# Hybrid decoder step: no drain of gathers between the later stages, 80 candidate sums instead of 256 in routing, and 24 gathered items moved between stages

## The chip, the cores and the metric

The kernel runs on one core of one Trainium2 chip. The metric is device time in microseconds (us) of one execution. The core has five engines: PE (matrix products), DVE (vector work), ACT (scalar work and activations), POOL (GpSimd; here it issues the gathers) and SP (here it only issues transfers). All transfers share the core's 16 DMA engines.

## The reference, cut to what matters

One decoder layer over 560 tokens (32 sample, 16 meta, 512 prompt), all in float32. The part before the experts is a norm, a large projection, eight gated-delta heads and eight attention heads, and an output projection. Then comes PEER, a retrieval of single experts, and most of the time goes there:

```python
qry = (xi @ w_query).reshape(PEER_BLOCK, PEER_HEADS, 2, PEER_HALF)
s = jnp.einsum('thpc,pnc->thpn', qry, sub_keys)
s1, i1 = lax.top_k(s[:, :, 0], PEER_TOPK)             # 16 of 128
s2, i2 = lax.top_k(s[:, :, 1], PEER_TOPK)
cand = (s1[..., :, None] + s2[..., None, :])          # 16 x 16 sums
cidx = (i1[..., :, None] * PEER_KEYS + i2[..., None, :])
top_s, pos = lax.top_k(cand, PEER_TOPK)               # 16 of 256
idx = jnp.take_along_axis(cidx, pos, axis=-1)
gate = jax.nn.softmax(top_s, axis=-1)
hid = jax.nn.gelu(jnp.einsum('td,thkd->thk', xi, expert_u[idx]), approximate=False)
return jnp.einsum('thk,thkd->td', (gate * hid), expert_v[idx])
```

Each token reads, for each of 8 heads, 16 rows of `expert_u` and 16 rows of `expert_v`, each row 2048 float32. Since the kernel works on 128 tokens at once, one *item* is one gather of 128 rows of 8 KB (1 MB) and one pass of DVE over it.

## The kernel before

The tokens are worked in two groups: `FIRST` (tag a, two tiles of 128 tokens) and `LATER` (tag b, tiles of 128, 128 and 48). Each group goes through the same five stages in `front`: `norm_and_gates`, `heads`, `mix_out` (output projection), `ffn_norm` and `route`. After `LATER`'s `route`, `rest_of_experts` does what is left of the experts.

A stage is a block in which each engine has its own instruction stream, ordered by semaphores. At the end of a block all engines meet; then `phase`'s `clear` resets the stage's semaphores, one barrier of all engines for each run of neighbouring numbers. `nc.Block()` ends with a drain on POOL: POOL waits there for the transfers that it has issued.

The experts are 1088 items, kept by `Stream` in a fixed order: 448 belong to tokens of `FIRST` (their indices are `known` once `FIRST` is routed), 640 to those of `LATER`. An item of kind u multiplies the gathered rows with the token's vector and sums them (L1919); an item of kind v adds the weighted rows to the result (L1934; the first of a set is L1930). POOL issues gathers (L1841) into a ring of `RING` = 6 buffers: `Stream.gather` runs up to six items ahead of what DVE has been given, and before each one waits until the buffer's last item has been consumed.

The 448 known items are spread over the stages of `LATER`. The table `OVERLAP` says how many each stage takes, and `Share` divides a stage's quota evenly over its steps: norm 14 items in 3 steps (one a tile), heads 330 at even marks of its written order, out 48 in 24 steps (8 column groups by 3 tiles), ffn 8 in 3 steps, route 48 in 32 steps (8 heads by 4 parts). `share.take` puts the items of a step into DVE's stream at that place, so all DVE work behind them waits for them. With `FIRST` there is no stream (`NONE`).

`mix_out`: PE makes a 256-column group of one tile (L2017) and DVE adds it to the residual (L2044); weights of `out_b_w` come in pieces of 2 MB, two buffers. The last gather of each stage waits for the last item of the stage, so POOL always ends a stage with up to six gathers under way.

`route`, for each of 8 heads: PE projects the queries (L2203) and scores them against 128 keys, twice (L2211); ACT copies queries and scores out of PSUM. `top16` finds the best 16 on DVE by MAX8, FIND_INDEX8 and MATCH_REPLACE8, eight at a time. Its first use is on 128 scores; the second is on the 256 sums `cand` (L2280). Then the index of each of the 16 winners is looked up by comparing its row and its column number with 0 to 15 (`iota`), multiplying with the index table `atf` and summing (L2294, L2297, L2299), and the gate is a softmax whose exponential is on ACT (L2237). ACT works in order: after the scores of a head it waits for `centred`, the middle of DVE's work on that head, before it copies the next head's queries.

Of the kernel before, what the change touches and what calls it, by code (L numbers as in the profile page):

```python
# [22 lines left out]
ALU = mybir.AluOpType  # L23
# [6 lines left out]
P = 128  # L30
# [69 lines left out]
def constant_parts():  # L100
    r = np.arange(P)
    row, col = r[:, None], r[None, :]
    mixed = FIRST.rows[0]
    seq0 = np.where(r < NS, r // NQ, np.where(r < mixed, NB, -1 - r))
    same0 = (seq0[:, None] == seq0[None, :]) & (r < mixed)[:, None]
    upto, after = [(row <= col) & same0, row <= col], [(row > col) & same0, row > col]
    levels = [((row // b) % 2 == 1) & (col // b == row // b - 1) for b in LEVELS]
    first_keys = np.arange(mixed - NS)[None, :]
    parts = {
        "upto": np.concatenate(upto, 1),  # L110
        "after": np.concatenate(after, 1),
        "not_upto": np.concatenate([np.where(m, 0.0, NEG) for m in upto], 1),
        "not_after": np.concatenate([np.where(m, 0.0, NEG) for m in after], 1),
        "levels": np.concatenate(levels[:1] + [m.T for m in levels[1:]], 1),
        "ident": row == col,
        "ones": np.ones((P, P)),
        "causal": np.where(col > row, NEG, 0.0),
        "members": seq0[:, None] == np.arange(NB + 1)[None, :],
        "iota": np.broadcast_to(np.arange(TOPK)[None, :], (P, TOPK)),
        "eps": np.full((P, 1), EPS),  # L120
        "eps_q": np.full((P, 1), EPS * HD),
        "row": row,
        "valid": row < LATER.rows[-1],
        "causal_mixed": np.where((row >= NS) & (first_keys > row - NS), NEG, 0.0),
        "causal0": np.where(same0 & (col <= row) | (row >= NS), 0.0, NEG)[:, :NS],
        "batch_cols": np.broadcast_to((np.arange(NS)[None, :] // NQ == np.arange(NB)[:, None]).reshape(1, -1),
                                      (P, NB * NS)),
    }
    return {k: np.asarray(v, np.float32) for k, v in parts.items()}
# [60 lines left out]
def build(nc, ins, outs):  # L190
    with ExitStack() as ctx:
# [21 lines left out]
        def keep(stack, name, shape, dt=F32):  # L213
            mem[name] = stack.enter_context(nc.sbuf_tensor(name, shape, dt))
# [91 lines left out]
def norm_and_gates(nc, ins, outs, mem, scr, group, stream, quota):  # L306
    cst, xnT = mem["cst"], mem["xnT"]
    T, own, samples = group.n, group.own, group.samples
    ctx, sem, buf = phase(
        nc, f"norm_{group.tag}",  # L310
        "const_in first_in vec_rows_in narrow_in bias_in pages_in x_in0 x_in1 x_squared x_root x_scaled x_turned "
# [18 lines left out]
    with ctx:  # L330
# [245 lines left out]
def heads(nc, ins, outs, mem, scr, group, stream, quota):  # L576
# [15 lines left out]
    ctx, sem, buf = phase(  # L592
        nc, f"heads_{group.tag}",
        " ".join(f"w_in{s}" for s in range(W)) + " projected evacuated "
# [125 lines left out]
    with ctx:  # L720
        block = ctx.enter_context(nc.Block())

# [1239 lines left out]
def mix_out(nc, ins, mem, scr, group, stream, quota):  # L1962
# [11 lines left out]
    with ctx:  # L1974
# [3 lines left out]
        w_out = ins["w_out"][0].rearrange("(k p) c -> p k c", p=P)  # L1978
        block = ctx.enter_context(nc.Block())

# [68 lines left out]
def ffn_norm(nc, ins, outs, mem, scr, group, stream, quota):  # L2049
# [3 lines left out]
    ctx, sem, buf = phase(  # L2053
        nc, f"ffn_{group.tag}",
        "keys_in squared rooted reciprocals normed turned copied h_out xi_out0 xi_out1 keys_turned keys_copied",
# [6 lines left out]
    with ctx:  # L2062
        block = ctx.enter_context(nc.Block())

# [77 lines left out]
def route(nc, ins, mem, scr, group, stream, quota):  # L2142

    cst, xiT, skT = mem["cst"], mem["xiT"], mem["skT"]
    T, N = group.n, group.cols
    ctx, sem, buf = phase(
        nc, f"route_{group.tag}",
        "w_in0 w_in1 w_in2 w_in3 w_packed0 w_packed1 w_packed2 w_packed3 projected0 projected1 query_copied0 query_copied1 scored0 scored1 scores_copied0 scores_copied1 "
        "scores_read cleared dve_passed dve_order centred exped routed",
        {"w": ([P, 2, KT, P],), "q": ([P, 2, N],), "sc": ([P, T, 2, KEYS],), "top": ([P, T, 2, TOPK],),  # L2150
         "at": ([P, T, 2, TOPK], U32), "atf": ([P, T, 2, TOPK],), "cand": ([P, T, TOPK, TOPK],),
         "best": ([P, T, TOPK],), "pos": ([P, T, TOPK], U32), "pos2": ([P, 2, T, TOPK], U32),
         "posf": ([P, 2, T, TOPK],), "hot": ([P, T, TOPK, TOPK],), "pick": ([P, 2, T, TOPK],),
         "gate": ([P, T, TOPK],), "sum": ([P, T],), "rec": ([P, T],)},
        {"pq0": [P, BANK], "pq1": [P, BANK], "ps0": [P, BANK], "ps1": [P, BANK]},
# [14 lines left out]
    with ctx:  # L2170
        block = ctx.enter_context(nc.Block())

# [69 lines left out]
        def _(dve):  # L2242
# [26 lines left out]
            for h in range(HEADS):  # L2269
                order = Counter(dve, sem["dve_order"], h, 100)  # L2270
                share.take(dve, h * PARTS + 1)
                for s in range(2):
# [15 lines left out]

                order.mark(nc.vector.tensor_scalar(B.pos2[:, 0], B.pos[:], 4, None, ALU.logical_shift_right))
                order.mark(nc.vector.tensor_scalar(B.pos2[:, 1], B.pos[:], TOPK - 1, None, ALU.bitwise_and))  # L2290
                order.wait()
                order.link(nc.vector.tensor_copy(B.posf[:], B.pos2[:]))
                for s in range(2):
                    order.link(nc.vector.tensor_tensor(  # L2294
                        B.hot[:], B.posf[:, s].unsqueeze(3).to_broadcast([P, T, TOPK, TOPK]),
                        cst("iota").unsqueeze(1).unsqueeze(1).to_broadcast([P, T, TOPK, TOPK]), ALU.is_equal))
                    order.link(nc.vector.tensor_tensor(  # L2297
                        B.hot[:], B.hot[:], B.atf[:, :, s, :].unsqueeze(2).to_broadcast([P, T, TOPK, TOPK]), ALU.mult))
                    order.link(nc.vector.tensor_reduce(B.pick[:, s], B.hot[:], AX_X, ALU.add))  # L2299
                order.link(nc.vector.scalar_tensor_tensor(B.pick[:, 0], B.pick[:, 0], float(KEYS), B.pick[:, 1],  # L2300
                                                          ALU.mult, ALU.add))
                order.mark(nc.vector.tensor_copy(mem["idx_all"][:, group.own, h, :], B.pick[:, 0]))
                dve.wait_ge(sem["exped"], h + 1)
                order.link(nc.vector.tensor_reduce(B.sum[:], B.gate[:], AX_X, ALU.add))
                order.link(nc.vector.reciprocal(B.rec[:], B.sum[:]))
# [67 lines left out]
```

## Time and profile before

| | |
|---|---|
| runs | median 4594.33 us (4588.70, 4594.33, 4604.27) |
| profiled execution | 4603.0 us, span 4601.2 us |
| busy over the span | DVE 3369.4 us, PE 2388.2 us, POOL 2327.6 us, ACT 569.8 us |
| moved by DMA | 1513.69 MB, 329 GB/s over the span |
| group FIRST | start to 1200.7 us |
| group LATER, with 448 items beside it | 1201.7 to 2943.4 us |
| rest of the experts, 640 items | 2966.5 us to the end |

A row of a view has the duration of instructions in us or ns and, where a column says idle, how long the engine stood before them and who released it. An engine's idle time matters only where nothing else that is needed later was going on. DMA share is the mean busy share of the 16 DMA engines.

### The profile page before, as it was taken

To read this page: it belongs to the slowest core of one execution; us is meant where nothing else is said; L and a number is where in the kernel's file an instruction comes from. 1 tells how busy PE (TensorE), PEld (TensorE's weight loads), DVE (VectorE), ACT (ScalarE), POOL (GpSimd) and SP (SyncE) were. 2 spreads that over 40 slices of the span, in tenths; PEclk is the share of its full clock that TensorE was granted. 3 is DMA by queue.
4 is the path that set the end of the run, shared out by engine and by line. 5 is a ranking of instruction groups with operands and counts; after the bars stand their busy time and mean duration, and the time that the engine had idled before them with its cause. 6 is when DMAs were issued, how large, how long until landed. Compare 5 with 4: busy or idle time off the path is not lost. (4 is left out here: it accounts for less than half of the span.)

```text
span 4601.2 us, 35157 instructions
## 1 busy us (share of the span) xinstructions
PE 2388.2 (52%) x11713; PEld 1884.3 (41%) x11713; DVE 3369.4 (73%) x4421; ACT 569.8 (12%) x1322; POOL 2327.6 (51%) x1217
## 2 busy tenths in 40 slices
PE   6999999898488898888749555100000000000000
PEld 5888888777366666666537443000000000000000
DVE  2333323217779999989867589799998989999998
ACT  1222222201122222222200000000000000000000
POOL 1010101000246666545645222388887888888886
PEclk9999999899699999999869777555555555555555
DMA  6766666487779999999989764499999999999998
GB/s 176 225 202 191 198 202 207 149 287 230 273 278 401 401 397 412 400 381 399 372 337 419 265 234 184 173 420 422 418 422 396 414 414 422 422 417 418 413 412 353
DMA packets 443932, 1513.69 MB, mean 329 GB/s; under 512 B 42044, under 2 KB 276208, under 8 KB 277848
## 3 DMA queue, kind: packets, MB, share of 16 engines
q0 software_dynamic: 161840, 1158.85, 62.1%
q1 hardware_dynamic: 269240, 251.94, 17.2%
q10 hardware_dynamic: 12672, 100.67, 5.5%
q8 instruction: 93, 1.52, 0.1%
q14 instruction: 87, 0.71, 0.0%
HBM read 1384.96 MB, written 126.21 MB: 328 GB/s over the span
## 5 line engine op out<-in xcount | busy, mean ns | idle before, releaser
L1919 DVE CUSTOM_DVE_ANT_0 ex_ring<-ex_ring,ex_xi 128x2048 f32<-128x2048 f32 x544 | 1243.6, 2290 | 129.3 <-DMA ex_ring<-in_peer_u_dram,ex_idx_s 40.0
L1934 DVE SCALAR_TENSOR_TENSOR ex_y<-ex_ring,ex_wt,ex_y 128x2048 f32<-128x2048 f32 x538 | 1264.6, 2351 | 96.2 <-DMA ex_ring<-in_peer_v_dram,idx_all 53.7
L1841 POOL DMA_INDIRECT ex_ring<-in_peer_v_dram,idx_all x384 | 811.8, 2114 | 255.9 <-DVE ex_y L1934 138.2
L1841 POOL DMA_INDIRECT ex_ring<-in_peer_u_dram,idx_all x384 | 782.6, 2038 | 293.6 <-DVE ex_hid L1919 187.5
L848 PE MATMUL heads_b_pj<-xnT_b,lead 128*128 128x304 f32 x2048 | 604.4, 433 | 7.2 <-PEq L270 3.7
L1873 PE MATMUL ex_fold<-ex_y,const 128*32 128x512 f32 (+1 forms) x48 | 24.3, 670 | 1110.8 <-DVE ex_y L1934 1038.9
L1873 PEld LDWEIGHTS ex_fold<-ex_y,const 128*32 128x32 f32 (+1 forms) x48 | 6.2, 134 | 1128.4 <-DVE ex_y L1934 1039.8
L1841 POOL DMA_INDIRECT ex_ring<-in_peer_v_dram,ex_idx_s x160 | 303.0, 1894 | 296.0 <-DVE ex_y L1934 218.1
L1841 POOL DMA_INDIRECT ex_ring<-in_peer_u_dram,ex_idx_s x160 | 319.2, 1995 | 224.3 <-DVE ex_hid L1919 181.0
L848 PEld LDWEIGHTS heads_b_pj<-xnT_b,lead 128*128 128x128 f32 x2048 | 377.2, 197 | 119.4 <-issue 17.3
L848 PE MATMUL heads_a_pj<-xnT_a,heads_a_w 128*128 128x256 f32 x1216 | 316.6, 398 | 1.9 <-DMA heads_a_w<-in_w_in_dram 1.9
L848 PEld LDWEIGHTS heads_a_pj<-xnT_a,heads_a_w 128*128 128x128 f32 x1216 | 226.7, 199 | 32.3 <-issue 2.9
L1891 ACT ACTIVATE ex_act<-ex_hid 128x16 f32<-128x16 f32 x34 | 7.3, 216 | 1721.0 <-DVE ex_hid L1919 1720.9
L848 PE MATMUL heads_a_pj<-xnT_a,lead 128*128 128x256 f32 x832 | 214.9, 398 | 3.5 <-PEq L270 3.5
L1837 POOL DMA_DIRECT2D ex_xi<-xi_scratch x13 | 7.0, 549 | 380.6 <-POOLq L270 315.1
L848 PEld LDWEIGHTS heads_a_pj<-xnT_a,lead 128*128 128x128 f32 x832 | 156.3, 200 | 24.7 <-issue 5.8
L2017 PE MATMUL out_b_acc<-out_b_w,mixT_b 128*128 128x256 f32 (+1 forms) x672 | 147.4, 380 | 0.0
L2017 PEld LDWEIGHTS out_b_acc<-out_b_w,mixT_b 128*128 128x128 f32 (+1 forms) x672 | 111.5, 168 | 35.8 <-issue 5.1
L1663 POOL DMA_DIRECT2D out_k_prompt_dram<-heads_a_f_kN x16 | 8.9, 560 | 220.8 <-ACT heads_a_f_kN L1282 220.8
L1645 POOL TENSOR_TENSOR heads_a_ub<-heads_a_uN,const 128x1024 f32<-128x1024 f32 x8 | 15.3, 1914 | 191.1 <-ACT heads_a_uN L1239 191.1
L2017 PE MATMUL out_a_acc<-out_a_w,mixT_a 128*128 128x256 f32 x448 | 99.4, 384 | 6.7 <-DMA out_a_w<-in_w_out_dram 6.7
L1651 POOL DMA_DIRECT2D out_gdn_sample_dram<-heads_a_sout x8 | 7.6, 950 | 186.1 <-DVE heads_a_sout L1511 186.1
(566 smaller groups left out, 4023.8 us busy)
## 6 DMA issues: line engine op xcount, KB each, us to landing
lead<-w_scratch SPq DMA_DIRECT2D x64, 1024.0 KB
heads_a_w<-in_w_in_dram SPq DMA_DIRECT2D x38, 1024.0 KB, 6.1
w_scratch<-heads_a_w ACTq DMA_DIRECT2D x38, 1024.0 KB, 4.1
lead<-in_w_in_dram SPq DMA_DIRECT2D x26, 1024.0 KB, 5.8
w_scratch<-lead ACTq DMA_DIRECT2D x26, 1024.0 KB, 4.4
out_a_w<-in_w_out_dram SPq DMA_DIRECT2D x7, 2048.0 KB, 14.2
w_out_scratch<-out_a_w ACTq DMA_DIRECT2D x7, 2048.0 KB, 9.0
out_b_w<-w_out_scratch SPq DMA_DIRECT2D x7, 2048.0 KB, 12.7
```

Of the source, the lines that this page charges most:

```text
L848: last = nc.tensor.matmul(pj[j % PJ][:, 0:N], slot(j)[:, k, :], xnT[:, k, :], start=(k == 0), stop=(k == KT - 1))
L1645: nc.gpsimd.tensor_tensor(B.ub[:], B.uN[:, 0, :].unsqueeze(1).to_broadcast([P, NB, HD]), cst("members", 0, NB).unsqueeze(2).to_broadcast([ ...
L1651: pool.dma_start(outs["gdn_sample"][0, :, h].rearrange("b k v -> k b v"), B.sout[:]).then_inc(sem["gs_out"], 16)
L1663: pool.dma_start(out[place, h, :], rows[own_rows, t, :]).then_inc(sem[f"{own}_out{t}"], 16)
L1837: pool.dma_start(self.tokens(s)[part.on, :], self.xi_rows[part.xi_rows]).then_inc(self.sem["xi_in"], 16)
L1841: pool.indirect_dma_start(self.ring[:, i % RING, :], None, self.tables[which], bass.IndirectOffsetOnAxis(ap=self.index(s, g, k), axis=0)). ...
L1873: last = self.nc.tensor.matmul(self.fold[0:rows, c:c + BANK], self.mem["cst"]("ident", r * rows, (r + 1) * rows), self.sum_of(s)[:, c:c + ...
L1891: self.nc.scalar.activation(self.act[:, g % 2, :], self.hid[:, g % 2, :], ACT.Gelu).then_inc(self.sem["activated"], 1)
L1919: nc.vector.tensor_tensor_reduce(ring, ring, self.tokens(s)[:], 1.0, 0.0, ALU.mult, ALU.add, self.hid[:, g % 2, k:k + 1]).then_inc(self.se ...
L1934: nc.vector.scalar_tensor_tensor(y, ring, wt, y, ALU.mult, ALU.add).then_inc(self.sem["consumed"], 1)
L2017: last = nc.tensor.matmul(acc[0:b - a, i, 0:GW], mixT[:, k, a:b], weights[:, k, :], start=(k == 0), stop=(k == KT - 1))
```

## The change

Three edits. First, from the `LATER` group on (`mem["gathering"]`), stages end without POOL's drain and their semaphores are cleared by SP followed by one barrier on semaphores only. Second, `route` (in both groups) forms 80 sums instead of 256: the whole of row 0 (16), columns 0 to 7 of rows 1 to 7 (56), and column 0 of rows 8 to 15 (8). No other sum can be among the best 16, as the scores are sorted. A position among the 80 needs a little more arithmetic to become a row and a column; the table of row indices has 17 entries, the first of them twice. The copy of the indices to float moves to ACT (three copies), the softmax's subtraction and sum move into ACT's exponential (one per tile), and the index goes to `idx_all` directly. Third, the quotas: 12 items leave heads and 12 leave route; 8 go to norm, 12 to out, 4 to ffn.

```diff
-        "iota": np.broadcast_to(np.arange(TOPK)[None, :], (P, TOPK)),
+        "iota": np.broadcast_to(np.arange(TOPK + 1)[None, :], (P, TOPK + 1)),
...
         for a, b in zip(starts, ends):
-            nc.all_engine_barrier(sems_to_clear=range(a, b))
+            if gathering:
+                nc.sync.sem_clear(range(a, b))
+            else:
+                nc.all_engine_barrier(sems_to_clear=range(a, b))
+        if gathering:
+            nc.all_engine_barrier(sem_only=True)
...
-OVERLAP = {"norm": 14, "heads": 330, "out": 48, "ffn": 8, "route": 48}
+OVERLAP = {"norm": 22, "heads": 318, "out": 60, "ffn": 12, "route": 36}
...
-        block = ctx.enter_context(nc.Block())
+        block = ctx.enter_context(nc.Block(no_gpsimd_drain=mem["gathering"]))
...
-                act.wait_ge(sem["centred"], h + 1)
-                nc.scalar.activation(B.gate[:], B.gate[:], ACT.Exp).then_inc(sem["exped"], 1)
+                act.wait_ge(sem["scores_read"], h + 1)
+                if h >= 1:
+                    act.wait_ge(sem["picked"], h)
+                nc.scalar.copy(B.table[:, 0, :, 0:1], B.at[:, :, 0, 0:1])
+                nc.scalar.copy(B.table[:, 0, :, 1:], B.at[:, :, 0, :])
+                nc.scalar.copy(B.table[:, 1, :, 0:TOPK], B.at[:, :, 1, :]).then_inc(sem["tabled"], 1)
+                act.wait_ge(sem["best_found"], h + 1)
+                nc.scalar.mul(B.neg[:], B.best[:, :, 0], -1.0).then_inc(sem["negated"], 1)
+                act.wait_ge(sem["negated"], h + 1)
+                for t in range(T):
+                    last = nc.scalar.activation(B.gate[:, t, :], B.best[:, t, :], ACT.Exp, bias=B.neg[:, t:t + 1],
+                                                accum_out=B.sum[:, t:t + 1])
+                last.then_inc(sem["exped"], 1)
...
-                order.mark(nc.vector.tensor_copy(B.atf[:], B.at[:]))
-                order.link(nc.vector.tensor_tensor(B.cand[:], B.top[:, :, 0, :].unsqueeze(3).to_broadcast([P, T, TOPK, TOPK]),
-                                                   B.top[:, :, 1, :].unsqueeze(2).to_broadcast([P, T, TOPK, TOPK]), ALU.add))
-                top16(order, [(B.cand[rows[t], t].rearrange("p a b -> p (a b)"), B.best[rows[t], t, :], B.pos[rows[t], t, :])
-                              for t in range(T)])
-
-                nc.vector.tensor_tensor(B.gate[:], B.best[:], B.best[:, :, 0:1].to_broadcast([P, T, TOPK]), ALU.subtract
-                                        ).then_inc(sem["centred"], 1)
+                first, second = B.top[:, :, 0, :], B.top[:, :, 1, :]
+                order.mark(nc.vector.tensor_tensor(B.cand[:, :, 0:TOPK], first[:, :, 0:1].to_broadcast([P, T, TOPK]), second, ALU.add))
+                order.mark(nc.vector.tensor_tensor(
+                    B.cand[:, :, TOPK:72].rearrange("p t (a b) -> p t a b", b=8),
+                    first[:, :, 1:8].unsqueeze(3).to_broadcast([P, T, 7, 8]),
+                    second[:, :, 0:8].unsqueeze(2).to_broadcast([P, T, 7, 8]), ALU.add))
+                order.mark(nc.vector.tensor_tensor(B.cand[:, :, 72:CANDS], first[:, :, 8:], second[:, :, 0:1].to_broadcast([P, T, 8]),
+                                                   ALU.add))
+                order.wait()
+                if h >= 1:
+                    dve.wait_ge(sem["exped"], h)
+                top16(order, [(B.cand[rows[t], t, :], B.best[rows[t], t, :], B.pos[rows[t], t, :]) for t in range(T)])
+                dve.sem_inc(sem["best_found"], 1)
                 share.take(dve, h * PARTS + 3)
...
+                order.mark(nc.vector.scalar_tensor_tensor(B.last[:], row, 9.0, column, ALU.is_equal, ALU.mult))
+                order.mark(nc.vector.tensor_scalar(B.second[:], row, 1.0, 8.0, ALU.is_equal, ALU.mult))
+                order.wait()
+                order.mark(nc.vector.tensor_tensor(B.place[:, 0], row, B.last[:], ALU.add))
+                order.mark(nc.vector.tensor_tensor(B.place[:, 1], column, B.last[:], ALU.subtract))
+                order.wait()
+                order.link(nc.vector.tensor_tensor(B.place[:, 1], B.place[:, 1], B.second[:], ALU.add))
+                dve.wait_ge(sem["tabled"], h + 1)
```

The look-up behind it is as before, with 17 columns for the first index and 16 for the second; the copy to `idx_all` and the sum of the gates on DVE are gone.

## Rows read from the trace of the kernel before

**Rows 1.** The page: busy time of each engine over the span.

```profile
PE 2388.2 (52%) x11713; PEld 1884.3 (41%) x11713; DVE 3369.4 (73%) x4421; ACT 569.8 (12%) x1322; POOL 2327.6 (51%) x1217
```

**Rows 2.** Busy time in stretches: FIRST's route, norm, heads, drain, out, drain, ffn, drain, route, drain, tail.

```profile
core 0: us, PE busy (x) PEld busy (x) DVE busy (x) ACT busy (x) POOL busy (x), PEclk, DMA share, GB/s
1038.30:1200.70 162.40, 124.75 (x576) 107.65 (x576) 125.73 (x524) 15.22 (x57) 0.00 (x0) 0.91 0.64 207
1201.70:1274.50 72.80, 30.03 (x168) 27.43 (x169) 45.23 (x64) 11.30 (x16) 33.63 (x21) 0.55 0.89 342
1274.50:2358.40 1083.90, 904.61 (x4304) 656.36 (x4304) 977.99 (x1098) 270.08 (x588) 643.25 (x331) 0.93 0.95 384
2358.40:2376.80 18.40, 0.00 (x0) 0.00 (x0) 0.00 (x0) 0.04 (x1) 2.66 (x3) 0.50 0.68 285
2376.80:2553.10 176.30, 171.21 (x768) 129.38 (x768) 118.31 (x98) 1.67 (x3) 84.52 (x51) 0.98 0.97 395
2553.10:2565.10 12.00, 0.00 (x0) 0.00 (x0) 0.00 (x0) 0.00 (x0) 1.73 (x2) 0.51 0.49 180
2565.10:2599.90 34.80, 9.15 (x48) 8.33 (x48) 31.02 (x30) 7.96 (x10) 12.78 (x6) 0.55 0.79 294
2599.90:2611.50 11.60, 0.04 (x1) 0.07 (x1) 0.07 (x1) 0.00 (x0) 1.87 (x2) 0.50 0.73 271
2611.50:2943.40 331.90, 167.61 (x608) 119.53 (x608) 283.54 (x774) 20.39 (x76) 74.01 (x46) 0.74 0.50 181
2943.40:2966.50 23.10, 0.09 (x1) 0.12 (x2) 0.00 (x0) 0.00 (x0) 5.53 (x6) 0.50 0.77 315
...
3010.00:3500.00 490.00, 0.00 (x0) 0.00 (x0) 456.04 (x308) 1.29 (x6) 425.78 (x197) 0.50 1.01 421
```

**Rows 3.** DVE's u items and POOL's gathers: ns, minimum, median and maximum.

```profile
L1919 DVE CUSTOM_DVE_ANT_0 ex_ring<-ex_ring,ex_xi x544: 2266/2291/2366, 1211.2 to 4499.8; 128x2048 f32<-128x2048 f32 x182
L1841 POOL DMA_INDIRECT ex_ring<-in_peer_u_dram,idx_all x384: 932/2232/6452, 1203.1 to 4490.8; - x192
```

**Rows 4.** In order of time, from heads to out: start us, us, what, idle before.

```profile
2356.03 2.35 DVE L1934 SCALAR_TENSOR_TENSOR ex_y<-ex_ring,ex_wt,ex_y 128x2048 f32<-128x2048 f32 x1 [0.45 <-DMA ex_ring<-in_peer_v_dram,ex_idx_s]
...
2360.73 0.93 POOL L1841 DMA_INDIRECT ex_ring<-in_peer_v_dram,ex_idx_s  x1 [0.30 <-issue]
...
2376.95 23.22 PE L2017 MATMUL out_b_acc<-lead,mixT_b 128*128 128x256 f32 x93 [27.44 <-PEq L270]
```

**Rows 5.** The same, from route to the rest of the experts.

```profile
2949.51 0.94 POOL L1841 DMA_INDIRECT ex_ring<-in_peer_u_dram,idx_all  x1 [0.30 <-issue]
...
2966.52 2.29 DVE L1919 CUSTOM_DVE_ANT_0 ex_ring<-ex_ring,ex_xi 128x2048 f32<-128x2048 f32 x1 [23.13 <-PEq L270]
...
2993.31 2.29 DVE L1919 CUSTOM_DVE_ANT_0 ex_ring<-ex_ring,ex_xi 128x2048 f32<-128x2048 f32 x1 [0.15 <-DMA ex_ring<-in_peer_u_dram,idx_all]
```

**Rows 6.** DVE's instructions in LATER's route by shape: count, busy us, mean ns.

```profile
L2262 DVE FIND_INDEX8 route_b_at<-route_b_top,route_b_sc 128x8 uint32<-128x128 f32 x64 | 17.1, 285 | 0.0
L2262 DVE FIND_INDEX8 route_b_pos<-route_b_best,route_b_cand 128x8 uint32<-128x256 f32 x32 | 13.0, 419 | 0.0
```

**Rows 7.** In order of time, DVE in LATER's route: no wait ahead of the second, one ahead of the third.

```profile
2655.34 0.18 DVE L2289 TENSOR_SCALAR route_b_pos<-route_b_pos 128x48 uint32<-128x48 uint32 x1
2655.44 0.18 DVE L2290 TENSOR_SCALAR route_b_pos<-route_b_pos 128x48 uint32<-128x48 uint32 x1
2655.65 0.21 DVE L2292 CAST route_b_posf<-route_b_pos 128x96 f32<-128x96 uint32 x1
```

**Rows 8.** In order of time, DVE in norm.

```profile
1241.52 0.15 DVE L446 RECIPROCAL norm_b_rs<-norm_b_rt 48x1 f32<-48x1 f32 x1 [3.85 <-ACT norm_b_rt L412]
...
1262.07 0.35 DVE L462 COPY norm_b_narrow<-norm_b_nar 128x24 f32<-128x24 f32 x3 [5.64 <-PE norm_b_nar L515]
```

**Rows 9.** DVE's waits for DMA in out: us in total, times, longest.

```profile
DVE ex_y L1934 <- DMA ex_ring<-in_peer_v_dram,ex_idx_s: 16.5, 7, 5.8
DVE ex_ring L1919 <- DMA ex_ring<-in_peer_u_dram,ex_idx_s: 11.7, 4, 5.5
```

More of the change, by code:

```diff
@@ L47 @@
 KEYS = 128
+CANDS = 80
 SEGS = 4
@@ L309, in norm_and_gates @@
     ctx, sem, buf = phase(
-        nc, f"norm_{group.tag}",
+        nc, mem["gathering"], f"norm_{group.tag}",
         "const_in first_in vec_rows_in narrow_in bias_in pages_in x_in0 x_in1 x_squared x_root x_scaled x_turned "
@@ L592, in heads @@
     ctx, sem, buf = phase(
-        nc, f"heads_{group.tag}",
+        nc, mem["gathering"], f"heads_{group.tag}",
         " ".join(f"w_in{s}" for s in range(W)) + " projected evacuated "
@@ L720, in heads @@
     with ctx:
[L721 removed]
+        block = ctx.enter_context(nc.Block(no_gpsimd_drain=mem["gathering"]))
         @block.sync
@@ L2053, in ffn_norm @@
     ctx, sem, buf = phase(
-        nc, f"ffn_{group.tag}",
+        nc, mem["gathering"], f"ffn_{group.tag}",
         "keys_in squared rooted reciprocals normed turned copied h_out xi_out0 xi_out1 keys_turned keys_copied",
@@ L2146, in route @@
     ctx, sem, buf = phase(
-        nc, f"route_{group.tag}",
+        nc, mem["gathering"], f"route_{group.tag}",
         "w_in0 w_in1 w_in2 w_in3 w_packed0 w_packed1 w_packed2 w_packed3 projected0 projected1 query_copied0 query_copied1 scored0 scored1 scores_copied0 scores_copied1 "
-        "scores_read cleared dve_passed dve_order centred exped routed",
+        "scores_read cleared dve_passed dve_order tabled picked best_found negated exped routed",
         {"w": ([P, 2, KT, P],), "q": ([P, 2, N],), "sc": ([P, T, 2, KEYS],), "top": ([P, T, 2, TOPK],),
-         "at": ([P, T, 2, TOPK], U32), "atf": ([P, T, 2, TOPK],), "cand": ([P, T, TOPK, TOPK],),
+         "at": ([P, T, 2, TOPK], U32), "table": ([P, 2, T, TOPK + 1],), "cand": ([P, T, CANDS],),
          "best": ([P, T, TOPK],), "pos": ([P, T, TOPK], U32), "pos2": ([P, 2, T, TOPK], U32),
-         "posf": ([P, 2, T, TOPK],), "hot": ([P, T, TOPK, TOPK],), "pick": ([P, 2, T, TOPK],),
-         "gate": ([P, T, TOPK],), "sum": ([P, T],), "rec": ([P, T],)},
+         "posf": ([P, 2, T, TOPK],), "last": ([P, T, TOPK],), "second": ([P, T, TOPK],), "place": ([P, 2, T, TOPK],),
+         "hot": ([P, T, TOPK, TOPK + 1],), "pick": ([P, 2, T, TOPK],),
+         "gate": ([P, T, TOPK],), "neg": ([P, T],), "sum": ([P, T],), "rec": ([P, T],)},
         {"pq0": [P, BANK], "pq1": [P, BANK], "ps0": [P, BANK], "ps1": [P, BANK]},
@@ L2290, in _ @@
-                order.mark(nc.vector.tensor_scalar(B.pos2[:, 1], B.pos[:], TOPK - 1, None, ALU.bitwise_and))
+                row, column = B.posf[:, 0], B.posf[:, 1]
+                order.mark(nc.vector.tensor_scalar(B.pos2[:, 0], B.pos[:], 3, None, ALU.logical_shift_right))
+                order.mark(nc.vector.tensor_scalar(B.pos2[:, 1], B.pos[:], 7, None, ALU.bitwise_and))
                 order.wait()
                 order.link(nc.vector.tensor_copy(B.posf[:], B.pos2[:]))
+                order.mark(nc.vector.scalar_tensor_tensor(B.last[:], row, 9.0, column, ALU.is_equal, ALU.mult))
@@ L2293, in _ @@
                 for s in range(2):
+                    n = TOPK + 1 - s
+                    hot, shape = B.hot[:, :, :, 0:n], [P, T, TOPK, n]
                     order.link(nc.vector.tensor_tensor(
-                        B.hot[:], B.posf[:, s].unsqueeze(3).to_broadcast([P, T, TOPK, TOPK]),
-                        cst("iota").unsqueeze(1).unsqueeze(1).to_broadcast([P, T, TOPK, TOPK]), ALU.is_equal))
+                        hot, B.place[:, s].unsqueeze(3).to_broadcast(shape),
+                        cst("iota", 0, n).unsqueeze(1).unsqueeze(1).to_broadcast(shape), ALU.is_equal))
@@ L2297, in _ @@
                     order.link(nc.vector.tensor_tensor(
[L2298 to L2302, printed above, removed]
+                        hot, hot, B.table[:, s, :, 0:n].unsqueeze(2).to_broadcast(shape), ALU.mult))
@@ L2303, in _ @@
+                    order.link(nc.vector.tensor_reduce(B.pick[:, s], hot, AX_X, ALU.add))
+                dve.sem_inc(sem["picked"], 1)
+                order.mark(nc.vector.scalar_tensor_tensor(mem["idx_all"][:, group.own, h, :], B.pick[:, 0], float(KEYS),
+                                                          B.pick[:, 1], ALU.mult, ALU.add))
                 dve.wait_ge(sem["exped"], h + 1)
-                order.link(nc.vector.tensor_reduce(B.sum[:], B.gate[:], AX_X, ALU.add))
                 order.link(nc.vector.reciprocal(B.rec[:], B.sum[:]))
```

13 lines of the change are left out of this document (7 added, 6 removed).

## The prediction, made before the changed kernel was run

> **What bounds the kernel now.** I read the engines' busy times first: DVE has most, 3369.4 of 4601.2 us, but no engine is busy throughout [rows 1], so I cut the span into stages [rows 2]. The reader is to see which column is nearly full in each. In the tail it is DMA (share 1.01 at 421 GB/s): 490 us for 197 gathers, 2.49 us each, while an item costs DVE only 2.29 us (kind u) or 2.35 (kind v) [rows 2 to 4]. The tail's 640 items stay 640, so the tail only moves; all that can be won lies before it. In heads DVE is the fullest: 978 of 1084 us, PE 905, DMA 0.95. In out PE (171 of 176 us) and DMA (0.97) are both nearly full and DVE has room. In route DVE works 284 of 332 us at half of the DMA. Between stages stand stretches of 18.4, 12.0, 11.6 and 23.1 us in which no engine computes and DMA runs dry [rows 2]. A move of items pays where it takes them off a full DVE and lays them on one that waits, if DMA can bring them.
>
> Sums are made against the profiled execution (4603.0 us); it lies 8.7 us above the median of the runs, so the forecast for the median is 4594.3 less the same saving.
>
> **The drains.** After heads DVE's last item ends at 2358.4, POOL's last issue at 2361.7, and the next stage starts at 2376.9 [rows 4]. POOL's issue has to end first in either kernel; the 15 us behind it are the ring of six gathers landing (6 x 2.49 = 14.9). FIRST's route ends without gathers and norm begins 1.0 us later (1200.7 to 1201.7), so a bare boundary costs about 1 us. What goes is 15.2 - 1.0 = 14 us. After out and ffn I keep 3 us (last issue and boundary): 12.0 - 3 = 9 and 11.6 - 3 = 8.6. After ffn SP also waits until the last `xi_scratch` rows have landed, in company of gathers; I take 7. Route to tail: POOL's sixth issue ends at 2950.5, DVE starts at 2966.5 [rows 5]. Without the drain it starts near 2951.5, and since gathers then never pause, the first item that waits for DMA (2993.3, the twelfth behind the start) comes at 2942.6 (first issue) + 2 for the landing + 14 transfers of 1 MB (the tokens and 13 gathers) x 2.49 = about 2979.5: 14 us. Norm to heads: POOL is long done there; 0. Bounds for all: 30 (others' waits stand in the same place) and 50 (every idle stretch to 1 us, with DMA never dry). Together 14 + 9 + 7 + 14 = 44.
>
> What is late next: a stage now starts with its ring in flight instead of landed, five gathers of debt. It costs nothing in out (below, inside the volume), and some in ffn.
>
> **80 sums, LATER's route.** A search over 256 columns takes 419 ns, over 128 it takes 285 [rows 6]: 1.05 ns a column, so 176 fewer save 0.185 us. A head has 3 tiles x (2 MAX8 + 2 FIND_INDEX8 + 1 MATCH_REPLACE8) = 15 of them: -2.8. The one sum of 768 columns (about 0.15 + 768 x 0.00105 = 0.95 us) becomes three of 48, 168 and 24, about 0.55: -0.4. Gone are two casts, the subtraction and the sum over the gates, and one wait: three at the 0.10 to 0.12 us step of instructions without a wait between, two at the 0.21 to 0.25 of those with one [rows 7]: -0.7. New are five small ones in three waits, +0.86, and 48 more columns on three passes of the look-up, +0.15. Net -2.9 a head, -23 for eight. DVE gives this back one to one only if it stays the bound: PE has 168 us in 332 [rows 2], 21 a head, against DVE's new 33 a head. ACT's extra steps (three copies, a negation, two more exponentials, about 1 us) lie beside DVE's look-up of over 6 us.
>
> **80 sums, FIRST's route.** Two tiles: ten searches, -1.87; the sum -0.2; -0.65; +0.95: -1.8 a head, -14. DVE is full there (126 of 162 us, most of the rest the start), with a period of 18.1 us; PE has 125 us, 15.6 a head, so a period of 16.3 still holds. This one is near: bounds -8 (PE, or ACT's longer chain in front of the next query copy, takes over) and -18.
>
> By the Trainium skill, "Vector Engine (DVE): Perf Modes", the section on the fixed extra latency of SBUF sources, many small instructions each pay a fixed cost exposed between them, and more than 512 columns are advised; this speaks against cutting one sum into three and adding five small steps. If each of the eight new ones cost its full 0.2 us, the two routes would save some 31 instead of 37 us, an estimate; the steps of 0.10 us without a wait [rows 7] say that much of that cost overlaps.
>
> **The items.** *Route* loses 12 at 2.24 to 2.35 us, on its full engine: -27. *Heads* loses 12: at 2.3 us -27.6 if DVE bounds all of it; PE is 83% busy and catches up a little, so -25, bounds -10 and -30. *Norm* gains 8 x 2.3 = 18.4 us on DVE, which stands idle 3.9 us before the last tile and 5.6 behind the last items [rows 8]; those fill: +9.5, bounds +8 and +14 (the small `c_scratch` store then also shares DMA with gathers). *Out* gains 12. DVE has room for them (118 of 176 us busy) but it waited for DMA there 28 us already [rows 9]; by volume, 176.3 us x 395 GB/s = 69.6 MB, and 12 gathers make it 82.2 MB, at 422 GB/s 195 us: +19, with a pause at the change of token set +20. Bounds +0 (PE sets the pace) and +30 (12 x 2.49). *Ffn* gains 4 x 2.3 = 9.2, and its first items now wait for gathers that share DMA with 5 MB of stores: +13, bounds +9 and +16.
>
> **Sum.** -14 (FIRST's route) + 9.5 - 25 - 14 + 20 - 9 + 13 - 7 - 27 - 23 - 14 = -90.5. 4603.0 - 90.5 = 4512.5; on the median 4594.3 - 90 = **4504**. The whole has room for it: of the time between 1201.7 and 2966.5 DMA was idle about 260 us by its shares [rows 2], and only 90 are taken.
>
> **Rivals.** *A: the moved items give nothing back where they leave heads.* PE (905 of 1084) or the written order sets heads; -10 there, and norm, out and ffn at their upper bounds +14, +30, +16. Against it: DVE is at 90%, PE at 83%. -14 + 14 - 10 - 14 + 30 - 9 + 16 - 7 - 27 - 23 - 14 = -58: 4536. *B: out swallows its 12 items* at PE's pace (+0 to +8) and heads gives 28: about -108: 4486. *C: the drains stay* in another form (POOL or SP still waits at the boundary): 44 less, 4548; the start of norm 1 us behind FIRST's route speaks against it. *D, the other side: PE loses its clock in out.* Granted 0.98 there, but 0.50 in the drains and 0.74 in route where PE is half busy [rows 2]. If waits for DMA brought out to the low level (1.2 GHz), a group of 7.0 us becomes 14: +168 in place of +20, 4652; it decides from the 13th of the 24 slow groups on. Against it: heads holds 0.93 at 83% busy, and out would be at 87%. *E: POOL becomes the bound.* A gather's issue takes 0.93 us alone, but a median of 2.23 and up to 6.45 beside DVE's work [rows 3]. If it averaged 4.5 in out, 60 x 4.8 = 288 us instead of 196: 4596, no gain. Against it: 84.5 us for 51 issues there, 1.7 each. The Trainium skill, "GPSIMD Engine Reference", key points, says that GpSimd shares its SBUF interfaces with VectorE and contends with DVE instructions of two SBUF inputs, as both kinds of item are; out is to have more of them per us, and by that rule alone issues get longer, not shorter.
>
> **How the numbers follow.** My forecast 0.58 (own range 4490 to 4522); A 0.15; B 0.13; C 0.06; D 0.03; E 0.03; 0.02 for something not seen. The range leaves out C's far half, D, E and little of B: **4478 to 4546**. A difference under 0.3% (14 us) is about what a measurement of this kernel can't tell from none: faster 0.94, same 0.03, slower 0.03.
>
> **What would show it.** Idle of the next stage's PE or DVE of 3 to 4 us behind each of heads, out and ffn, and DVE's first item of the tail under 10 us behind POOL's first issue of it; MAX8 and its kin at 80 columns near 235 ns; LATER's route 283 us, FIRST's 148; heads near 1059, out near 196, norm near 82, ffn near 48; the tail's length from its twelfth item unchanged. The prediction is wrong if heads doesn't shorten by about two items' time in each head, if out costs 30 or nothing, or if some DVE or PE instruction waits longer at a stage's start for a transfer that stands behind six gathers.

## The result, and the profile after

The changed kernel takes 4516.88 us (median of 4 runs, 4514.75 to 4520.94) against 4592.04 us of the kernel before (4588.70 to 4604.27). The ratio is 0.9833, 95% interval [0.9813, 0.9853]: 75 us less. The forecast of 4504 was 13 us too low, and its range of 4478 to 4546 holds the time. The profiled execution took 4517.43 us (span 4515.7) beside 4603.0 (span 4601.2) before, 85.5 us less. Of the 13 us, 5 are thus the sum's (85.5 for 90.5). The other 8 come from carrying the saving of one execution over to the medians: the one before lay 8.7 us above the median shown with it, this one 0.5 above its own.

Busy times (page) and the stretches in the order of [rows 2] up to the tail, of the changed kernel:

```profile
PE 2382.3 (53%) x11713; PEld 1887.7 (42%) x11713; DVE 3336.9 (74%) x4469; ACT 584.6 (13%) x1446; POOL 2327.1 (52%) x1217
```

```profile
core 0: us, PE busy (x) PEld busy (x) DVE busy (x) ACT busy (x) POOL busy (x), PEclk, DMA share, GB/s
1032.50:1180.50 148.00, 120.02 (x576) 104.31 (x576) 111.49 (x548) 23.56 (x113) 0.00 (x0) 0.93 0.70 228
1181.50:1270.60 89.10, 31.08 (x168) 27.81 (x169) 63.83 (x80) 12.83 (x18) 51.50 (x29) 0.52 0.98 373
1270.60:2328.10 1057.50, 902.62 (x4304) 663.41 (x4304) 950.02 (x1076) 263.83 (x582) 614.71 (x319) 0.92 0.95 381
2328.10:2329.80 1.70, 0.02 (x1) 0.05 (x1) 0.02 (x1) 0.22 (x1) 1.40 (x2) 0.50 0.98 410
2329.80:2535.30 205.50, 176.19 (x768) 131.80 (x768) 145.78 (x116) 1.50 (x3) 116.30 (x65) 0.92 1.01 412
2535.30:2536.50 1.20, 0.00 (x0) 0.00 (x0) 0.03 (x1) 0.00 (x0) 0.90 (x2) 0.50 1.00 416
2536.50:2580.30 43.80, 9.27 (x48) 8.33 (x48) 40.04 (x36) 7.96 (x10) 21.15 (x11) 0.58 1.00 414
2580.30:2581.40 1.10, 0.03 (x1) 0.07 (x1) 0.00 (x1) 0.00 (x0) 0.94 (x1) 0.50 0.93 171
2581.40:2874.80 293.40, 168.47 (x608) 120.05 (x608) 234.01 (x780) 31.56 (x148) 43.81 (x35) 0.76 0.48 172
2874.80:2881.40 6.60, 4.21 (x6) 1.00 (x7) 0.04 (x1) 0.00 (x0) 5.08 (x6) 0.54 0.98 389
```

DVE is still the engine with most work, 3336.9 us for 3369.4 [rows 1]. The empty stretches between stages are down to 1.7, 1.2 and 1.1 us. Next read DMA's share, the last column but one: norm went from 0.89 to 0.98, out from 0.97 to 1.01, ffn from 0.79 to 1.00. DMA is now nearly full or full where the items went. The table sets the stages against the prediction, from one stage's first instruction to the next one's; a stage holds the boundary behind it.

| stretch | before, us | after, us | difference | predicted |
|---|---|---|---|---|
| start to FIRST's route (same code) | 1038.3 | 1032.5 | -5.8 | 0 |
| FIRST's route | 163.4 | 149.0 | -14.4 | -14 |
| norm | 72.8 | 89.1 | +16.3 | +9.5 |
| heads | 1102.4 | 1059.1 | -43.3 | -25 - 14 |
| out | 188.2 | 206.8 | +18.6 | +20 - 9 |
| ffn | 46.3 | 44.8 | -1.5 | +13 - 7 |
| LATER's route to POOL's first gather of the tail | 331.2 | 292.7 | -38.5 | -27 - 23 |
| from there to the end | 1658.6 | 1641.7 | -16.9 | -14 |
| sum | | | -85.5 | -90.5 |

How far single stretches vary is seen from the runs below. In the fourteen traces of this study the stretch ahead of FIRST's route takes 1032.5 to 1039.0 us with the same code, and heads with the new quotas and no drain took 1053.4 to 1059.1 in five. Four terms are off by more than that: norm by 7, out by 8 (+18.6 for +11), ffn by 8 the other way (-1.5 for +6) and LATER's route by 11.5. The trace of the kernel before is itself a long one, 8.7 us above its median; kernel 3 below, whose heads are the same, took 1098.1 us there for its 1102.4.

Three stretches in order of time, DVE and POOL of the changed kernel. First from heads to out [rows 4]:

```profile
2325.77 2.35 DVE L1947 SCALAR_TENSOR_TENSOR ex_y<-ex_ring,ex_wt,ex_y 128x2048 f32<-128x2048 f32 x1 [0.76 <-DMA ex_ring<-in_peer_v_dram,ex_idx_s]
...
2348.10 0.42 DVE L2057 TENSOR_TENSOR hres_b<-hres_b,out_b_acc 128x256 f32<-128x256 f32 x1 [19.98 <-DMA hres_b<-in_x_prompt_dram]
...
2330.49 0.94 POOL L1854 DMA_INDIRECT ex_ring<-in_peer_v_dram,ex_idx_s  x1 [0.30 <-issue]
2351.54 2.27 POOL L1854 DMA_INDIRECT ex_ring<-in_peer_u_dram,ex_idx_s  x1 [20.12 <-DVE ex_hid L1932]
```

DVE's first residual add stands 18.3 us behind the stage's start (2329.8). DVE idled for 20.0 us, until the rows of `hres_b` had landed, whose loads were issued at 2329.76 behind a ring of gathers. POOL waits as long. Before, the add stood 10.1 us behind the start, and waited for PE. This is the sign that my last paragraph named; experiment 6 says what it costs.

Then the change of token set in LATER's route (DVE, then POOL):

```profile
2629.61 2.35 DVE L1947 SCALAR_TENSOR_TENSOR ex_y<-ex_ring,ex_wt,ex_y 128x2048 f32<-128x2048 f32 x1 [0.23 <-DVEq L170]
...
2647.81 1.28 DVE L1943 TENSOR_SCALAR ex_y<-ex_ring,ex_wt 128x2048 f32<-128x2048 f32 x1 [15.77 <-DMA out_y_prompt_dram<-ex_y]
...
2642.52 0.85 POOL L1874 DMA_DIRECT2D out_y_prompt_dram<-ex_y  x1 [7.82 <-DMA out_y_prompt_dram<-ex_y]
```

The first row is item 415, the last of its set; the second is item 416, which overwrites `ex_y` and waits until the set's rows are stored. The store is two transfers that the kernel puts one behind the other: POOL issued the second (third row) after a wait of 7.8 us for the first. With 36 items over 32 steps they are taken in neighbouring steps, the end of one head and the start of the next, with nothing between. With the old 48 items a look-up lay between them, and DVE waited 9.7 us.

Then from route to the tail [rows 5]:

```profile
2873.98 1.66 POOL L1854 DMA_INDIRECT ex_ring<-in_peer_u_dram,idx_all  x1 [0.30 <-issue]
...
2881.36 2.29 DVE L1932 CUSTOM_DVE_ANT_0 ex_ring<-ex_ring,ex_xi 128x2048 f32<-128x2048 f32 x1 [6.58 <-DMA ex_ring<-in_peer_u_dram,idx_all]
```

The tail's first item starts 7.4 us behind POOL's first issue. Last, the searches over 80 columns, for the 419 ns over 256 in [rows 6]: ns minimum, median and maximum:

```profile
L2294 DVE FIND_INDEX8 route_b_pos<-route_b_best,route_b_cand x48: 225/234/238, 2615.5 to 2858.3; 128x8 uint32<-128x80 f32 x32, 48x8 uint32<-48x80 f32 x16
```

### The profile page after: what moved, and what is told of

It reads as the page before. It is cut to its first block and busy times, and to the rows that moved or that the text cites. A ratio compares the mean times of both kernels' runs of the same rounds, so it can differ in the third digit from the quotient of the medians.

```text
span 4515.7 us, 35346 instructions
## 1 busy us (share of the span) xinstructions
PE 2382.3 (53%) x11713; PEld 1887.7 (42%) x11713; DVE 3336.9 (74%) x4469; ACT 584.6 (13%) x1446; POOL 2327.1 (52%) x1217
## 3 DMA queue, kind: packets, MB, share of 16 engines
q1 hardware_dynamic: 269240, 251.94, 17.5%
## 5 line engine op out<-in xcount | busy, mean ns | idle before, releaser
L1854 POOL DMA_INDIRECT ex_ring<-in_peer_v_dram,idx_all x384 | 802.7, 2090 | 258.2 <-DVE ex_y L1947 147.8
L1854 POOL DMA_INDIRECT ex_ring<-in_peer_u_dram,ex_idx_s x160 | 335.5, 2097 | 168.6 <-DVE ex_hid L1932 114.6
L2030 PE MATMUL out_b_acc<-out_b_w,mixT_b 128*128 128x256 f32 (+1 forms) x672 | 152.7, 389 | 14.9 <-DVE hres_b L2057 13.3
```

The source lines that it names most:

```text
L1854: pool.indirect_dma_start(self.ring[:, i % RING, :], None, self.tables[which], bass.IndirectOffsetOnAxis(ap=self.index(s, g, k), axis=0)). ...
L2030: last = nc.tensor.matmul(acc[0:b - a, i, 0:GW], mixT[:, k, a:b], weights[:, k, :], start=(k == 0), stop=(k == KT - 1))
```

## The experiments

**1 to 4: each part alone, and the change without its quotas.** 1 is the kernel before with this line alone; 4 is the changed kernel without it.

```diff
-OVERLAP = {"norm": 14, "heads": 330, "out": 48, "ffn": 8, "route": 48}
+OVERLAP = {"norm": 22, "heads": 318, "out": 60, "ffn": 12, "route": 36}
```

2 takes the boundaries from the changed kernel and all else from the kernel before; 3 takes the 80 sums and keeps drains and quotas as before.

> The kernel before with only the quotas changed (22, 318, 60, 12, 36); drains and 256 sums stay. Theory: what heads (-26) and route (-27, less 6 for a set's end that now meets DVE with nothing between) give is paid back in norm (+15), out (+21) and ffn (+9): about -2, between -8 and +6 us. Rival, as predicted before the result: norm +9.5, out +20 and ffn +9 leave -14 or more.

4599.11 us (4590.04 to 4604.4, 11 runs), ratio 1.0013 [1.0004, 1.0022]: 6 us slower, the upper edge of my theory; the rival's -14 is out. By stage, against the kernel before: norm +17.4, heads -33.4, out +27.5, ffn +8.8, LATER's route up to POOL's first gather of the tail -20.2. DVE waited 15.8 us for the store at the change of set. With the drains kept, out's twelve items thus cost 27.5 us already.

> The kernel before with only the drains and barriers changed, old quotas, 256 sums. Theory: four idle stretches go (about -16, -11, -10, -16), and 8 us come back in out, where the first residual add waits for rows that stand behind six gathers: about -44, between -38 and -50. Rival (the debt is paid back in each next stage): -25 or less in size.

4548.33 us (4543.6 to 4551.68), ratio 0.9905 [0.989, 0.992]: 44 us less. Out itself, without the boundary, takes 178.6 us for 176.3: 2 us came back there, not the 8 of my theory.

> The kernel before with only the routing changed to 80 sums, drains and old quotas stay. Theory: -14 in the first group's route and -21 to -23 in the later group's: -35, between -30 and -40. Rival: in the later route PE and ACT take part of it, -25 or less in size.

4551.86 us (4548.65 to 4559.64), ratio 0.9916 [0.9902, 0.9929]: 40 us less. By stage: FIRST's route 149.0 for 163.4, LATER's 309.6 for 331.2, of which 2.8 is a shorter wait at the change of set (6.9 for 9.7). That is the upper edge of my theory.

> The changed kernel with the old quotas (14, 330, 48, 8, 48): the sum of the two edits above, -75 to -85, so as fast as the changed kernel (4517 +- 8 us) or a little faster. Rival: the moved items are needed to use what the missing drains free, then this is 10 us or more slower than the changed kernel.

4508.9 us (4507.06 to 4516.68), ratio 0.9819 [0.9805, 0.9832]: 83 us less, 8 under the changed kernel. The edits are worth -44 and -40 and add up; the move of 24 items costs 6 to 8 us where I had it at 9.5 us of gain (+9.5 - 25 + 20 + 13 - 27). By stage, 4 against the changed kernel: norm 72.6 and 89.1, heads 1085.3 and 1059.1, out 179.8 and 206.8, ffn 35.9 and 44.8, route up to POOL's first gather of the tail 310.9 and 292.7. An item costs 2.1, 2.2, 2.2 and 2.2 us in the first four, and gives back only 1.5 in route.

Kernels 3 and 4 differ by the drains alone: heads 1098.1 and 1085.2, out 187.0 and 179.8, ffn 45.4 and 35.9, tail 1655.4 and 1643.4 us.

**5: the change of set put apart.**

```diff
-"ffn": 12, "route": 36
+"ffn": 11, "route": 37
```

> The changed kernel with one item moved from ffn (12 to 11) to LATER's route (36 to 37), so that the last item of a token set (number 415) and the first one that must wait for the set's rows to be stored (416) are taken on both sides of a top-16 search of 8.4 us, not one behind the other. My theory (what the new quotas lose over the old ones is mostly this stall: 15.8 us, against 7.1 with the old quotas and 15.8 again in the kernel before with the new quotas alone): the stall falls to about 7 and the time by 6 to 9 us, to about 4509. Rival (the wait only moves: items then wait for something else behind it, and the quotas lose their 8 us in norm and out): within 2 us of the changed kernel, 4515 to 4519.

4512.71 us (4509.97 to 4516.04), ratio 0.9825 [0.9811, 0.9838].

```profile
2651.81 1.29 DVE L1943 TENSOR_SCALAR ex_y<-ex_ring,ex_wt 128x2048 f32<-128x2048 f32 x1 [7.82 <-DMA out_y_prompt_dram<-ex_y]
```

The wait fell from 15.8 to 7.8. Route took 287.6 us for 292.7 with an item more, ffn 42.6 for 44.8: together -7.3, as expected. In the whole time it is -4, between theory and rival and with an interval that overlaps the changed kernel's; the stages show the cause, the totals only agree with it.

**6: DVE's wait in out filled with items.**

```diff
 def _(dve):
+    share.take(dve, 3 if stream else 0)
     dve.wait_ge(sem["x_in"], 16 * len(parts))
```

> The changed kernel; in out DVE takes seven items before it waits for the rows of hres, instead of behind the second item, so that the 20.0 us wait is filled with 16 us of items. If DVE's late start is what out pays for the missing drain (the first residual add came 10.2 us behind the stage's start before, and 18.3 after): 8 to 14 us less, about 4505. Rival, which I hold the likelier: DMA is at a share of 1.00 or more in every part of out in the changed kernel, so its volume (84.9 MB at 412 GB/s) sets the stage and DVE's wait costs nothing of its own: 0 to 3 us less, out still near 205 us.

4518.18 us (4513.32 to 4526.66), ratio 0.9839 [0.9824, 0.9855]. The rival holds: out takes 209.5 us, not less than 206.8, though DVE no longer waits for the rows. It waits 50.5 us for gathers instead of 39.9. Its row of the windows:

```profile
core 0: us, PE busy (x) PEld busy (x) DVE busy (x) ACT busy (x) POOL busy (x), PEclk, DMA share, GB/s
2324.30:2533.00 208.70, 175.38 (x768) 131.24 (x768) 145.86 (x116) 1.60 (x3) 112.02 (x66) 0.93 0.99 405
```

A wait of 20 us on the engine with most work, and nothing is lost by it. That DMA sets out's length instead fits its share of 0.99 to 1.01 and experiment 11 below.

**7: norm's eight items back to heads.**

```diff
-OVERLAP = {"norm": 22, "heads": 318,
+OVERLAP = {"norm": 14, "heads": 326,
```

> The changed kernel with the 8 items of norm given back to heads (norm 22 to 14, heads 318 to 326), so that all stages behind them take the same items as in the changed kernel. By my prediction's terms (8 items cost 9.5 us in norm and 8 x 2.1 = 16.7 in heads) this is 7 us slower: about 4524. By the traces (norm 16.4 us longer for its 8 items, heads 26.0 shorter for 12, so 17.3 for 8) it makes no difference: -2 to +3 us, 4515 to 4520.

4522.81 us (4516.55 to 4533.46), ratio 0.9848 [0.9831, 0.9866]. The whole alone would be taken for my prediction's 7 us. By stage it is the other: norm 72.5 for 89.1 (-16.6), heads 1072.6 for 1059.1 (+13.5; +16.5 against the median, 1056.1, of the five traces with 318 items and no drain there). The 5.6 us by which the spans differ lie ahead of norm, in code that is the same (6.2 us there). The eight items cost about as much in norm as in heads.

**8: both edits with old quotas.** Edit 6, and norm 14, heads 330, out 48, ffn 12, route 44.

> The version that the runs point to: no drains, 80 sums, norm 14, heads 330 and out 48 as in the kernel before, 12 items in ffn and 44 in LATER's route (which puts a top-16 search between items 415 and 416), and in out six items taken before the wait for the rows of hres. Against the changed kernel with the old quotas (4508.9), whose set-change stall is 7.1 us already: a theory in which every item costs its 2.25 us wherever it is taken gives 0 to -3, 4506 to 4509; if the late wait in out is worth its 8 us there, where DMA is also full, 4500.

4522.92 us (4510.8 to 4524.33), ratio 0.9839 [0.9823, 0.9855]. A miss: 14 above kernel 4, which ran on another chip (8 above kernel 10, the same version on a third). The two spans differ by 6.3 us: ffn +9.0 for its four items, LATER's route only -4.7 for the four it gives (1.2 of the shortfall is the wait, 8.3 for 7.1), and in code and items that are the same FIRST's route +2.9, heads -4.7, out +1.8, the tail +2.0. The rest of the 14 is not explained.

**9 and 10: the changed kernel and kernel 4 once more, on one chip.**

> The changed kernel as it is, on the same chip and in the same rounds as the three runs beside it, and a second trace of it. 4512 to 4521 us. What the new quotas cost is then its difference to the next run, without a change of chip between them.

4525.18 us (4508.88 to 4528.1), ratio 0.984 [0.982, 0.986].

> The changed kernel with the quotas of the kernel before, again, beside the changed one. My theory (in four of five stages an item costs the same 2.2 us wherever it is taken, and the new quotas lose only at the change of token set in LATER's route: 15.8 us of waiting against 7.1): 6 to 9 us under the run before this one. Rival (the 8 us between the two in the runs so far are the difference of two chips and of code that did not change, ahead of FIRST's route, where profiled executions vary by 6 us): within 3 us of it.

4514.98 us (4511.09 to 4515.59), ratio 0.982 [0.9806, 0.9833]: 10 us less on the same chip, near my theory's 6 to 9, though the intervals still overlap. Over all runs of the two versions the medians are 4519.84 (9 runs) and 4511.5 (10 runs), 8 apart. The wait at the change of set is 16.8 us in kernel 9 and 6.8 in kernel 10. By stage, 9 against 10: norm +17.1, heads -30.4, out +24.9, ffn +8.9, route -17.5, together +3. Kernel 10's out:

```profile
core 0: us, PE busy (x) PEld busy (x) DVE busy (x) ACT busy (x) POOL busy (x), PEclk, DMA share, GB/s
2343.40:2524.80 181.40, 171.83 (x768) 129.77 (x768) 118.10 (x98) 1.53 (x4) 88.02 (x54) 0.97 1.01 410
```

Out's DMA share is 1.01 with 48 items already, once the drains are gone.

**11: one drain kept, at the end of heads.**

```diff
 # in heads
-block = ctx.enter_context(nc.Block(no_gpsimd_drain=mem["gathering"]))
+block = ctx.enter_context(nc.Block())
```

> The changed kernel with POOL's drain kept at the end of heads alone; 16.7 us of empty time return between heads and out. My theory: the ring of six gathers that lands in that time (5.2 MB) no longer lands in out, where DMA is full (share 1.01), so out gets shorter by 6 to 12 us and the whole is slower by 5 to 11, 4522 to 4528. Rival, my prediction's step (the five gathers in flight cost out nothing): out stays at 205 us and the whole is 14 to 17 us slower, 4531 to 4534.

4526.65 us (4522.02 to 4528.63), ratio 0.9847 [0.9833, 0.986]. Against the changed kernel on the same chip that is +1.5, against its first runs +10, so the whole doesn't decide. The windows of heads' drain and of out do:

```profile
core 0: us, PE busy (x) PEld busy (x) DVE busy (x) ACT busy (x) POOL busy (x), PEclk, DMA share, GB/s
...
2328.00:2345.80 17.80, 0.00 (x0) 0.00 (x0) 2.51 (x3) 0.00 (x0) 4.08 (x3) 0.50 0.74 299
2346.80:2548.00 201.20, 174.68 (x768) 131.08 (x768) 145.90 (x116) 1.56 (x3) 114.90 (x63) 0.94 0.99 399
```

Out is 4.9 us shorter (201.7 for 206.6, the mean of the changed kernel's two traces), its volume 80.3 MB (201.2 us x 399 GB/s) for 84.7 (205.5 x 412). The other traces with 60 items there and no drain took 207 to 209.5. Heads with its boundary is 1069.9 us for 1059.1 and 1054.0, 13.3 more than their mean. So of the 13 us that the drain costs there, out gives back 5, and 8 stay. That is a little under the 6 to 12 that my theory gave to out, inside its 5 to 11 for the whole, and not the nothing of the prediction's step.

**12: a tile of its own for the third set's sum.**

```diff
 def sum_of(self, s):
+    if s is self.sets[2]:
+        return self.y3
     return self.y2 if s.second else self.y
 # take(), ahead of the waits of a set's first v item
+    if s is self.sets[2]:
+        earlier = None
+    elif s is self.sets[3]:
+        earlier = self.sets[1]
 # front(), LATER: mixT and y3 live to the end
+    tokens = stream.outer if stream else own
+    stream.y3 = tokens.enter_context(nc.sbuf_tensor("ex_y3", [P, D], F32))
```

> The changed kernel, where the third token set has a tile of its own for its sum, so that item 416 waits for no store; the tile takes the place of nothing (mixT is kept to the end so that it finds room). If the 15.8 us wait is a loss of its own, in a stage where DMA is half idle and DVE the bound: 12 to 16 us less, about 4502. Rival (what DVE doesn't wait for there it waits for at the next gathers, since the ring stood still for the store): 3 to 8 us less, about 4511.

4505.82 us (4496.81 to 4512.33), ratio 0.9803 [0.9786, 0.982]: 19 us under the changed kernel on the same chip (4525.18), 11 under its first runs. Item 415, item 416 and the next search:

```profile
2630.27 2.35 DVE L1956 SCALAR_TENSOR_TENSOR ex_y<-ex_ring,ex_wt,ex_y 128x2048 f32<-128x2048 f32 x1 [0.23 <-DVEq L170]
...
2632.74 1.29 DVE L1952 TENSOR_SCALAR ex_y<-ex_ring,ex_wt 128x2048 f32<-128x2048 f32 x1
2633.94 1.24 DVE L2300 MAX8 route_b_top<-route_b_sc 128x8 f32<-128x128 f32 x6
```

Route up to POOL's first gather of the tail takes 276.9 us for 292.7: the whole 15.8 come back. This wait was a loss of its own, unlike the longer one in out, since here DVE is the bound (234 busy of 293 us) and DMA stands at 0.48. It has the lowest median of the study; its interval still overlaps kernel 10's.

## Why the prediction came out as it did

**The drains, 44: right.** Alone they are worth 44 us. Kernels 3 and 4 give, by stage, 12.9 after heads, 7.2 after out, 9.5 after ffn and 12.0 before the tail, for 14, 9, 7 and 14. Empty time went from 18.4 to 1.7, 12.0 to 1.2 and 11.6 to 1.1 us, less than the 3 us that I kept; the tail came 16.9 us nearer for 14.

**The debt of five gathers: wrong, but small.** "It costs nothing in out (below, inside the volume)": the volume was not complete. The 69.6 MB of before's out leave out what landed in the drain behind it, at its end [rows 2]; without drains out is filled at both ends. What the debt costs is seen where only drains change: out itself takes 175.3 us in kernel 3 and 178.6 in kernel 4, and experiment 11 gets 4.9 us back. So it is 3 to 5 us, and the boundary behind out, 1.2 us where I had kept 3, gives part of it back.

**Out's twelve items, +20: mis-sized.** They cost 27.5 us in kernel 1, where every drain stays, and 26.9 and 24.9 without drains (the changed kernel against 4, kernel 9 against 10). Kernel 1's out:

```profile
core 0: us, PE busy (x) PEld busy (x) DVE busy (x) ACT busy (x) POOL busy (x), PEclk, DMA share, GB/s
2359.50:2563.20 203.70, 173.13 (x768) 129.90 (x768) 145.91 (x116) 1.52 (x3) 118.28 (x64) 0.94 0.99 400
```

These are 81.5 MB (203.7 us x 400 GB/s), the volume that I forecast (82.2 MB), but at 400 GB/s and not at 422, which had made it 195 us. I had taken the rate of the full DMA for the whole stage. In its first 60 us kernel 1 moves only 340 to 362 GB/s (the kernel before 351 to 369), and 422 to 424 after that; what keeps gathers from filling that start is not shown. In the changed kernel it is 84.7 MB at 412 GB/s, 205.5 us: 6 us for 2.5 MB more than I had, 5 us for the rate. That the 20 us wait for `hres_b` rows is not the cause was shown by experiment 6. Ffn came out lower (-1.5 for +6: its items 8.9 us for 13, its drain 9.5 for 7), so that out and ffn together took +17.1 for +17. That this sum is right is luck.

**80 sums, FIRST's route, -14: right** (-14.4). **LATER's route, -23: mis-sized.** Alone it gave 21.6, with 2.8 of it the shorter wait for the store: -18.8. The searches are as forecast, 235 ns at 80 columns, and a head's sums and searches went from 7.9 to 4.8 us (-3.1 for -3.2). The rest of the look-up was to gain 0.7 and lose 1.0; it went from 7.5 us to 8.3. By the Trainium skill, "VectorE: DVE Perf Modes", on the fixed extra latency, small instructions cost more than their columns, which I had turned into 31 us for both routes in place of 37. Measured were 14.4 + 18.8 = 33, between the two, so the trace agrees with that rule in its direction, though FIRST's route alone shows nothing of it.

**The items: the step that failed in sign.** Heads gave 26.0 us (kernel 4 against the changed one), 30.4 (10 against 9) and 33.4 (before against 1) for the 25 that I forecast; part of the last is before's trace, 4 us longer there than kernel 3's. Norm was put at +9.5 on the ground that DVE stood idle there [rows 8]. Those two waits did shrink, from 7.3 to 3.5 us and from 5.6 to none, but waits for gathers grew from 0.5 to 5.5:

```profile
DVE ex_ring L1932 <- DMA ex_ring<-in_peer_u_dram,idx_all: 5.5, 13, 1.6
```

DVE's idle time in norm is 25.3 us (89.1 - 63.8) for 27.6: nothing much was filled, and +16.3 was paid. That the items cost there about what they cost in heads was shown by experiment 7. Why is argued only: DMA's share of 0.98 speaks for the transfers (2.49 us each); but the items also stand in DVE's stream in front of norm's own work, at 2.3 us each, and no run here tells the two apart. What failed is my "those fill": in norm, out and ffn an item costs 2.1 to 2.3 us, and heads gives 2.2 to 2.8 back.

**LATER's route, -27 for its items: mis-sized by a wait that I had not looked for.** DVE's busy time fell by 49.5 us (283.5 to 234.0), as -27 - 23 asks, but the stretch only by 38.5. Of the 11.5 missing, 6.1 are the longer wait at the change of set (15.8 for 9.7) and 4.2 the look-up above. With the old quotas in the changed kernel it was 7.1, so the new quotas pay 8.7 us for it (10.0 between kernels 9 and 10). That is as much as they cost in all, 6 to 10 us by the medians; by the five stages it is 8, 3 and 0 in the three pairs, so it can't be said more closely. Experiments 5 and 12 took the wait out in two ways and got back 7.3 and 15.8 in the stages, and kernel 12, with the new quotas, is 9 us under kernel 10, with the old.

**The sum.** 85.5 for 90.5 looks better than its terms: 5.8 us lie in code that is the same, so the stages that I forecast gave 79.7, and misses stand on both sides (norm, out and LATER's route 7 to 11 us short of the forecast, heads, ffn and tail 3 to 8 us better).

**Rivals.** A was nearer than my own terms on norm (+14, measured +16.3) and on out's items (+30, measured 25 to 27), and wrong on heads (-10). B: out didn't swallow its items. C, D and E didn't come: boundaries are bare; PE's granted clock in out is 0.92 for 0.98, and its busy time rose by 5.0 us, not by the 168 of D; POOL's issues fill 116.3 of 205.5 us in out, 1.8 each for 1.7 (84.5 us for 51). That is the direction of the rule of the Trainium skill, "GPSIMD Engine Reference", key points, which I had set beside it, and far from a bound.

## What to carry to other kernels

Work moved into a stage because its compute engine idles there cost its full price here (2.1 to 2.3 us an item, in stages at a DMA share of 0.89 and 0.97 before), so read the DMA column of the target, by parts of the stage, and count the bytes that used to land in the gap you remove. A new quota also moves which step meets a periodic event (here the store at the end of a set): list these events and see what stands between each and whoever waits. And price a wait by the bound of its stage: 20 us of DVE in a stage full of DMA cost nothing, 15.8 us in one bound by DVE cost 15.8.

## What the hardware showed that I had not expected

- Loads on SP's queue are held up by gathers on POOL's: the three loads of `hres_b` rows, 2.5 MB together, were issued at 2329.76 with some five gathers still in flight and complete at 2348.1. Behind a landed ring (kernels 1 and 11) DVE had them 10 us from the stage's start.
- DMA's rate at full share is not one number: 388 to 393 GB/s in the first 70 us of the changed kernel's out, and 422 to 424 in the rest, both at a share of 1.01 to 1.02. SP's loads are 11.9 of the 27.4 MB in the first part and 8.4 of 57.2 in the second. 2 MB weight pieces stand beside gathers in both, so they alone are not the reason; which it is isn't shown.
- Identical code took 1032.5 to 1039.0 us up to FIRST's route in different builds and executions, as much as the effects of experiments 5 and 7 on the whole; these could be read only from the stages.
